# A hybrid decoder step on one core: the order of the prologue's loads, first chunks and first norm

## The reference

```python
def rmsnorm(x, g):
    y = xf * lax.rsqrt(jnp.mean(xf * xf, axis=-1, keepdims=True) + EPS)
    return y * g
...
for l in range(DEPTH):
    mod = (jax.nn.silu(c) @ p['w_ada'][l] + p['b_ada'][l])[:, None, :]
    shift1, scale1, gate1, shift2, scale2, gate2 = jnp.split(mod, 6, axis=-1)
    h = rmsnorm(x, p['g_mix'][l]) * (1 + scale1) + shift1
    mix, nb_a, nb_c, nb_d, v_n = token_mixers(h, buf_a[l], buf_c[l], buf_d[l], start_pos, l, p)
    x = x + gate1 * mix
    h = rmsnorm(x, p['g_ffn'][l]) * (1 + scale2) + shift2
    ...   # dense SwiGLU in layer 0, top-2 of 8 experts in layer 1
    x = x + gate2 * f
y = rmsnorm(x, p['g_final'])
```

## Time and profile before

| | |
|---|---|
| median of 3 runs | 1662.54 us (1662.24 to 1664.62) |
| the profiled execution | 1664.16 us, of which the span from the first to the last instruction is 1662.4 |
| mean granted clock of TensorE | 0.969 of full speed |
| share of TensorE in the chain that ended last | 86% |
| first matmul of the first projection | 72.4 us after the span's start |

### The profile page before, as it was taken

One profiled execution on the slowest core, in us unless ns is written; L12 is line 12 of the kernel. 1 busy time (PEld: TensorE's weight loads), 2 busy tenths in 40 slices (PEclk: granted clock), 3 DMA queues, 4 the chain that ended last, 5 costly groups with the idle time before them and its releaser, 6 DMA issues.

```text
span 1662.4 us, 26743 instructions
## 1 busy us (share of the span) xinstructions
PE 1529.7 (92%) x11956; PEld 1446.6 (87%) x11956; DVE 476.6 (29%) x804; ACT 371.9 (22%) x622; POOL 417.0 (25%) x224
## 2 busy tenths in 40 slices
PE   7699989999999999999998975989989999999992
PEld 4499879899999999998997964989989998999991
DVE  1467562500111001126986331111110110010115
ACT  2322243322221222323224222111111110010114
POOL 0358135332343243525833402000000000000005
PEclk9899999999999999999999997999999999999996
DMA  7645242554254331333634075879878695648744
GB/s 231 196 140 166 77 127 82 177 153 131 80 138 126 102 102 52 97 120 103 172 107 127 7 238 182 275 241 342 274 252 300 216 345 180 209 160 295 250 161 173
DMA packets 291584, 286.90 MB, mean 173 GB/s; under 512 B 8109, under 2 KB 283199, under 8 KB 291414
## 3 DMA queue, kind: packets, MB, share of 16 engines
q1 hardware_dynamic: 203286, 230.23, 42.3%
q10 hardware_dynamic: 84400, 42.51, 9.4%
q0 software_dynamic: 3760, 12.09, 2.0%
HBM read 266.45 MB, written 19.07 MB: 172 GB/s over the span
## 4 chain that ended last, share of the span: by engine, by line
PE 86%; DVE 5%; DMA 3%; issue 2%; SPq 2%; ACT 1%; POOL 1%; POOLq 0%; ACTq 0%; DVEq 0%
PE PP L783 36%; PE PP L1109 22%; PE PP L1121 11%; PE PP L824 7%; PE PP L796 3%; PE PP L757 2%; PE PP L768 1%; DMA adaw<-in_w_ada 1%; PE PP L1080 1%; PE PP L1091 1%; DVE mem L1584 1%; DVE mem_r L1578 1%; PE PP L957 1%; SPq L508 1%; DVE stat L1569 1%
## 5 line engine op out<-in xcount | busy, mean ns | idle before, releaser
L783 PE MATMUL PP<-hT_r,mem_r 128*128 128x260 f32 x2624 | 435.8, 285 | 4.6 <-DVE xT L1596 3.2
L639 POOL TENSOR_TENSOR mem_r<-mem,mem_r 128x1024 fp32r<-128x1024 f32 (+1 forms) x108 | 318.0, 2960 | 471.8 <-ACT mem_r L1237 471.4
L1109 PE MATMUL PP<-big,mem 128*128 128x128 f32 (+4 forms) x2816 | 365.3, 293 | 20.7 <-issue 19.9
L1109 PEld LDWEIGHTS PP<-big,mem 128*128 128x128 f32 x2816 | 362.6, 195 | 22.5 <-issue 21.3
L783 PEld LDWEIGHTS PP<-hT_r,mem_r 128*128 128x128 f32 x2624 | 364.0, 188 | 11.7 <-issue 7.7
L783 PE MATMUL PP<-mem_r 128*128 128x260 f32 x1312 | 263.8, 283 | 0.0
L783 PEld LDWEIGHTS PP<-mem_r 128*128 128x128 f32 x1312 | 201.9, 188 | 0.0
L1121 PE MATMUL PP<-big,mem 128*128 128x128 f32 (+4 forms) x1408 | 185.4, 288 | 0.0
L1121 PEld LDWEIGHTS PP<-big,mem 128*128 128x128 f32 x1408 | 179.1, 191 | 0.0
L739 POOL DMA_INDIRECT mem<-y_by_expert,place x10 | 9.7, 974 | 606.1 <-SPq L586 603.4
L824 PE MATMUL PP<-adaw,cs 128*9 128x128 f32 x1280 | 148.1, 274 | 13.9 <-DMA adaw<-in_w_ada 9.0
(11 more groups left out here) (237 smaller groups left out, 1063.3 us busy)
## 6 DMA issues: line engine op xcount, KB each, us to landing
mem<-in_w_moe SPq DMA_DIRECT2D x48, 1536.0 KB, 9.1
mem<-in_w_moe SPq DMA_DIRECT2D x32, 1408.0 KB, 9.4
adaw<-in_w_ada ACTq DMA_DIRECT2D x80, 512.0 KB, 4.9
mem<-in_w_dense SPq DMA_DIRECT2D x20, 1024.0 KB, 5.5
mem<-in_w_in SPq DMA_DIRECT2D x16, 1024.0 KB, 5.6
mem<-in_w_moe SPq DMA_DIRECT2D x16, 1024.0 KB, 6.8
mem<-in_w_dense SPq DMA_DIRECT2D x16, 704.0 KB, 4.7
mem<-in_w_out SPq DMA_DIRECT2D x8, 1024.0 KB, 5.2
```

Of the source, the lines that this page charges most:

```text
L639: pool.tensor_tensor(r_(raw), raw, read_(hi), ALU.subtract).then_inc(w_lo, 1)
L783: mm = pe.matmul(PP[q][:, h, 0:HT], r_(w[:, k, :]), r_(x[:, k, HT * h:HT * h + HT]), start=(i == 0 and w is wh and x is hi), stop=(i == le ...
L1109: mm = pe.matmul(PP[w][:, f % 2, 0:n], raw[:, w, k, :], hn[:, k, 0:n], start=(k == 0), stop=(k == KD - 1))
```

## The change

SP issues `first_pair(0)` in front of x, and `first_pair(2)` in front of `mixer_loads`. TensorE multiplies pair 0's chunks in front of the transposes of x. VectorE's copies of the mixers' inputs for layer 0 move from ahead of the norm into it, ahead of tile 4. ScalarE's `first_rows(2)` moves to tile 2 and the rounding of the first two weight units to tile 4. GpSimd does the samples' columns of the first norm in two parts, tiles 0 to 5 after the fifth product and tiles 6 and 7 after the seventh; TensorE waits for the second part in front of the seventh tile.

```diff
         def norm_step(tag, k, n):
-            return ns[k], NORM_STEPS[k] * tag + n
+            return ns[k], NORM_STEPS[k] * tag + n + (1 if k == "hs" and tag else 0)
...
             sp.dma_start(rows[0:96, 2, :], A["b_ada"].rearrange("l (r p) -> (l r) p", p=P)).then_inc(b_in, 16)
+            first_pair(0)
             for t in range(4):
                 sp.dma_start(xin[:, t, :], A["x_prompt"][0, P * t:P * t + P, :]).then_inc(x_in, 16)
             sp.dma_start(xin[0:NS, 4, :], A["x_sample"].rearrange("b s d -> (b s) d")).then_inc(x_in, 16)
-            first_pair(0)
...
             first_pair(1)
+            first_pair(2)
             mixer_loads(0)
-            first_pair(2)
             sp.wait_ge(ada_mm, 2)
             first_pair(3)
...
             def norm_samples(tag, l, scale, shift):
                 split = tag < 3
-                if tag == 0:
-                    pool.wait_ge(*norm_step(0, "xhat", KD - 1))
-                xs, hi = xT[:, :, SEQ:T], hT[:, :, SEQ:T]
...
                 pool.wait_ge(*norm_step(tag, "rec", 1))
...
+                for j0, j1 in ((0, KD - 2), (KD - 2, KD)) if tag == 0 else ((0, KD),):
+                    if tag == 0:
+                        pool.wait_ge(*norm_step(0, "xhat", j1 - 1))
+                    xs, hi = xT[:, j0:j1, SEQ:T], hT[:, j0:j1, SEQ:T]
...
+                    last.then_inc(ns["hs"], 1)
...
                     if k == 0:
                         pe.wait_ge(*norm_step(tag, "hs", 1))
+                    if k == KD - 2 and tag == 0:
+                        pe.wait_ge(*norm_step(0, "hs", 2))
                     pe.wait_ge(*norm_step(tag, "h", k + 1))
...
             pe.wait_ge(pro_dve, 2)
+            for c in range(2):
+                first_chunk(0, c)
             pe.wait_ge(x_in, 16 * NT)
...
             tr.then_inc(pro_tr, 1)
-            for c in range(2):
-                first_chunk(0, c)
             pe.wait_ge(vec_in, 16 * NVEC)
...
                 if tag == 0:
                     first_rows(1)
-                    first_rows(2)
-                    upper(u)
-                    upper(u + 1)
...
                 for j in range(KD):
+                    if tag == 0 and j == 2:
+                        first_rows(2)
                     if tag == 0 and j == 4:
+                        upper(u)
+                        upper(u + 1)
                         first_rows(3)
                         for g in range(ADA_RING):
                             ada_load(g)
...
                 for j in range(KD):
+                    if tag == 0 and j == 4:
+                        mixer_copies(0)
                     if tag == 0 and j % 2 == 0:
                         first_pair(j // 2)
...
             for l in range(DEPTH):
+                if l:
+                    mixer_copies(l)
                 norm_dve(2 * l, l, SCALE1, SHIFT1)
```

More of the change, by code:

```diff
@@ L643, in norm_samples @@
                 split = tag < 3
-                if tag == 0:
-                    pool.wait_ge(*norm_step(0, "xhat", KD - 1))
-                xs, hi = xT[:, :, SEQ:T], hT[:, :, SEQ:T]
-                hs = hlo[:, :, SEQ:T] if split else hi
                 pool.wait_ge(*norm_step(tag, "rec", 1))
[L649 to L656, removed]
+                for j0, j1 in ((0, KD - 2), (KD - 2, KD)) if tag == 0 else ((0, KD),):
+                    if tag == 0:
+                        pool.wait_ge(*norm_step(0, "xhat", j1 - 1))
+                    xs, hi = xT[:, j0:j1, SEQ:T], hT[:, j0:j1, SEQ:T]
+                    hs = hlo[:, j0:j1, SEQ:T] if split else hi
+                    link(pool.tensor_tensor(hs, xs, stat[:, SEQ:T].unsqueeze(1).to_broadcast([P, j1 - j0, NS]), ALU.mult))
+                    link(pool.tensor_tensor(hs, hs, mod[:, l, 8 * scale + j0:8 * scale + j1, 1:NQ], ALU.mult))
+                    last = pool.tensor_tensor(hs, hs, mod[:, l, 8 * shift + j0:8 * shift + j1, 1:NQ], ALU.add)
+                    if split:
+                        link(last)
+                        link(pool.tensor_copy(r_(hi), hs))
+                        last = pool.tensor_tensor(r_(hs), hs, read_(hi), ALU.subtract)
+                    last.then_inc(ns["hs"], 1)
             for l in range(DEPTH):
@@ L1283, in norm_act @@
                 root(2, stat[:], D, ns["root"])
+                fill = FILL.get(("norm", tag), ())
                 if tag == 0:
                     first_rows(1)
-                    first_rows(2)
-                    upper(u)
-                    upper(u + 1)
                 elif tag < 3:
@@ L1291, in norm_act @@
                     upper(u + KD - 1)
-                fill = FILL.get(("norm", tag), ())
                 ada_rows(("norm", tag), fill[0:2])
                 for j in range(KD):
+                    if tag == 0 and j == 2:
+                        first_rows(2)
                     if tag == 0 and j == 4:
+                        upper(u)
+                        upper(u + 1)
                         first_rows(3)
@@ L1589, in norm_dve, with mixer_copies @@
                     lower(KD - 1)
+            def mixer_copies(l):
+                dve.wait_ge(*step(l, "ws_tr", 1))
+                dve.tensor_copy(wsT, PP[3][:, 0, :].rearrange("p (h t) -> p h t", h=4)).then_inc(s["ws_copy"], 1)
+                dve.wait_ge(*step(l, "st_tr", 1))
+                for dst, src, r in ((hisA, PP[3][:, 1, 0:32], 2), (hisC, PP[3][:, 1, 32:512], 30),
+                                    (hisD, PP[0][:, 0, 0:240], 15)):
+                    for ct in range(2):
+                        m = NS * r
+                        last = dve.tensor_copy(dst[:, ct, :, 0:r], src[:, ct * m:ct * m + m].rearrange("p (b r) -> p b r", r=r))
+                    last.then_inc(s["st_copy"], 1)
             def add_gated(l, sec, q, pair, free, up):
```

## The result

The changed kernel took 1650.73 us (median of 5 runs, 1649.32 to 1663.27) beside 1664.62 for the kernel before (5 runs). The ratio is 0.9916, 95% interval 0.9891 to 0.9941: 13.9 us less (9.8 to 18.1 by the interval), where 14.1 were forecast. Timed once more (further down), the same kernel gained 8.8 us (5.7 to 12.2), so the match of 13.9 with 14.1 is closer than these measurements can bear out. The profiled execution has a span of 1648.1, 14.3 less than before.

The account below looks back on a forecast made before the run. TensorE was taken to bound the kernel, its first products held up by a late first norm. An earlier start (−11.4) and the kept clock (−2.7) gave −14.1 us: 1648.4 against the median 1662.54, whole range 1646.4 to 1654.1.

Parts of the forecast that it names:

- The sum: First products start at 61.0 instead of 72.38 (−11.4) and take 11.78 instead of 14.44 (−2.7): together −14.1 us.
- the port's case: Rival, chance 0.23: VectorE holds up GpSimd's second `lower`; TensorE starts at 63.7, gain 8.7, time 1653.8.
- First chunks in front of x: Prologue, SP and TensorE: pair 0 ahead of x is worth nothing by itself, −0.1 to +1.0 us.
- Pair 2 in front of the mixer's loads: SP's queue: TensorE's 1.81 wait goes; pair 3 issued 37.3 to 39.3, W_in's first chunk at 49.3 to 51.3.
- The norm's tiles ahead of the copies: VectorE's first norm: reciprocal at 36.4, fifth tile at 56.4, last low part at 66.7 (before 71.63).
- Weights' halves and part one: GpSimd: two `lower` from 52.2 to about 57.0, samples of tiles 0 to 5 from 57.4, taking 3.35; TensorE at 61.0.
- Part two: GpSimd's samples of tiles 6 and 7 end at 68.7, hidden by 1.1 us before TensorE's seventh step.
- The clock: Before the first products TensorE idles only 1.8 us, so the granted clock is kept and 2.66 us aren't lost.

Follow-up runs that it names:

- the second trace: The changed kernel run once more, unaltered: median 1656.4 us, ratio 0.9947 to the kernel before.
- 24 products in front: Changed kernel plus 24 thrown-away products of the identity on TensorE ahead of pair 0's chunks: median 1661.4 us, ratio 0.9957 to the kernel before.

## Why the prediction was right, step by step

*The sum* held in the first trace: the start moved by 11.8 (forecast 11.4) and the products by 2.8 (2.7). The next products kept their 11.78. The time was 1650.7 for 1648.4, with the kernel before 2.1 higher too (1664.6 for 1662.5). That the number fits so closely is in part luck: in the second trace the start moved by 10.1 and the products by 1.3, and the second measurement of the gain, 8.8, is nearly that of the port's case (8.7), though by other steps. The path, tiles and samples that come early enough for TensorE to start near 61, held in both.

*First chunks in front of x* was mis-sized, and for its reason. "Worth nothing by itself" looked at TensorE's sums only: they ended at 34.85 for 34.1, since TensorE's first work behind 5.5 us of rest ran slowly: the chunks took 2.3 more, and x's transposes, which had come first before, 1.6 less. SP's side was missed: with the two large loads of pair 0 out first, the first small vector is issued in 0.31 us, where it takes 4.77 with x in front, and pair 1 leaves at 13.82 instead of 18.00. By E of single traces this is worth 2.0 to 5.2 us, the width being the changed kernel's own spread; by the timed ratio no worth is shown.

*Pair 2 in front of the mixer's loads*: chunk (2,0) no longer waited in any trace with this order. Pair 3 left at 39.04 (37.3 to 39.3), W_in was rounded from 51.19 (49.3 to 51.3) in the first trace, 53.21 in the second. The range of this term was too narrow by 2 us, and it is the term that now decides.

*The norm's tiles ahead of the copies*: the reciprocal stood at 37.11 for 36.4, and the rest followed: the fifth tile at 57.8 (forecast 56.4), the last low part at 66.9 (66.7).

*Weights' halves and part one* came out right by two errors that cancel in half. VectorE was held by 1.15 instead of at most 0.7, so that part one started 0.55 late; and its five operations took 2.36, near the 2.5 of the scaled row and not the 3.35 taken. The start came 0.44 ahead. Part two ended at 66.98, 1.7 ahead of the forecast.

*The rival of the port* named the right two engines and the wrong loser. `lower` kept its 4.66; VectorE's operation stood until `lower` had ended, 1.15 us in the first trace and 3.9 over two operations in the second. The rule of the Trainium skill that was set beside it (GPSIMD Engine Reference, section Specifications) says that the two contend, and here they did so at VectorE's cost.

*The clock* was kept in the first trace, but the reason given, a pause of 1.8 between one of 1.81 and one of 2.72, is no rule. It stayed at 1.00 behind 1.09 in the changed kernel, 1.07 with 24 products in front and 2.08 with the copies ahead of the norm; it fell behind 1.08 with pair 2 late, 1.09 with both moves undone, and 0.87 inside the kernel with 24 products. That TensorE had stood before doesn't decide it either: the 2.08 came after a stand of 7.94, in which the clock had fallen and behind which it had come back; and of two kernels with the same work and pauses up to the 0.87 one lost the clock there. What decides is open. So this term came true by luck, as far as the runs show; where the clock fell, the products took 1.4 to 2.7 us longer.

## What to carry to other kernels

Moving one engine's work earlier pays only up to the next thing that comes late: here the split and the copies had to move together, and undoing either of them took back more than half of what E had gained. Where several chains end within a microsecond of each other, one trace isn't the kernel: run the unchanged thing again before a difference is put down to an edit, and then give the latest chain (here W_in) slack. In a queue the order of large and small loads has a price of its own, to be read from how long the issues stand; whether it reaches the end is another question, and here the times don't show that it does.

## What the runs showed of the hardware

- TensorE's first work after 5 us of rest ran slowly with the granted clock at 1.00 in its rows: 32 matmuls of 128x256 took 8.7 to 9.7 us in seven traces, and 7.1 behind products that are thrown away. In the slow part a microsecond holds 4 of them, as many as where the clock reads 0.50 (both moves of SP undone, 46 to 47 us). The Trainium skill (TensorE: Matmul & The Clock Gate, part 1) says that a rested TensorE stands at the lower of its clocks by default; the pace agrees with that, the granted clock of these rows doesn't show it.
- The granted clock fell to 0.50 behind a pause of 0.87 us in one trace and stayed at 1.00 behind one of 2.08 in another.
- A two-input operation of VectorE that takes 0.18 us stood 1.33 beside GpSimd's `lower`, and ended with it; `lower` kept its 4.66 for two. In the second trace it stood 2.06, and the next, 0.75 alone, 2.78.
- The three `adaw` issues held ScalarE's queue for 2.35 us in the first trace and 4.02 in the second of one kernel.
